# Expert rows in lanes of 32-row units: ten static rounds in place of eleven in a mixture-of-experts decoder trunk

## What is computed

```
scores = sigmoid(h @ w_router)                      # 512 x 16
group  = argmax over 4 groups of (sum of its two best biased scores)
expert = top_k(scores in that group, 2)             # 2 experts for each token
gate   = scores[expert] / sum(scores[expert])
counts = bincount(expert)                           # 1024 assignments over 16 experts
yb     = (silu(xb @ w_gate[e]) * (xb @ w_up[e])) @ w_down[e]   # xb: the rows of expert e
out[tok] += gate * yb
```

## Time and profile before

| what | us |
|---|---|
| three runs | 1645.20, 1642.72, 1634.35; median 1642.72 |
| the profiled execution | 1631.18 |
| its span, first to last instruction | 1629.4 |
| mixture of experts, layer 0: first round's first matmul to last down product's end | 653.3 to 934.4 |
| the same, layer 1 | 1315.0 to 1596.7 |
| spacing of the static rounds | 22.61 |

### The profile page before, as it was taken

The page is one execution under the profiler, slowest core; times in us unless marked ns, Lnnn a source line. Parts: engine busy times, 40 slices in busy tenths (PEclk is TensorE's granted clock), DMA queues, the critical chain, the costliest instruction groups (busy, mean ns, idle before and its releaser), DMA issues.

```text
span 1629.4 us, 22551 instructions
## 1 busy us (share of the span) xinstructions
PE 1434.7 (88%) x9837; PEld 743.0 (46%) x9837; DVE 674.6 (41%) x1044; ACT 306.5 (19%) x500; POOL 71.5 (4%) x199
## 2 busy tenths in 40 slices
PE   5999999967878797899999859969998789999992
PEld 3445565536666545433333344535654353333331
DVE  2114334235677316432333235785643543332334
ACT  2121211123342103100000042221112400000002
POOL 7000000000000000000000010000000000000001
PEclk9899999987999898999999979989999989999997
DMA  9686674031000007999997761201100599989884
GB/s 343 219 293 198 207 242 146 1 116 41 3 3 32 24 0 279 404 424 375 353 426 294 273 244 52 78 26 52 52 0 0 233 374 400 386 339 421 335 348 168
DMA packets 91215, 334.17 MB, mean 205 GB/s; under 512 B 6521, under 2 KB 37485, under 8 KB 74733
## 3 DMA queue, kind: packets, MB, share of 16 engines
q1 hardware_dynamic: 76880, 287.94, 46.4%
q10 hardware_dynamic: 8476, 23.82, 3.7%
q0 software_dynamic: 5760, 20.97, 3.4%
HBM read 309.65 MB, written 23.07 MB: 204 GB/s over the span
## 4 chain that ended last, share of the span: by engine, by line
PE 74%; DVE 14%; DMA 6%; ACT 4%; issue 2%; POOL 0%; DVEq 0%; SPq 0%; ACTq 0%; POOLq 0%
PE banks L1736 18%; PE banks L1284 14%; PE banks L1758 10%; PE banks L1656 5%; DVE work L1872 4%; PE banks L1325 4%; PE banks L1273 3%; PE banks L1220 3%; DMA work<-in_w_down_dram 2%; PE banks L1640 2%; PE banks L1719 1%; DVE work L1878 1%; DMA work<-h_rows,idx_tok 1%; PE banks L1450 1%; DMA ring<-in_w_ada_dram 1%
## 5 line engine op out<-in xcount | busy, mean ns | idle before, releaser
L1284 PE MATMUL banks<-h_features,ring 128*128 128x512 f32 (+1 forms) x656 | 291.3, 599 | 5.6 <-ACT h_features L897 4.0
L1736 PE MATMUL banks<-ring,work 128*64 128x512 f32 x672 | 231.3, 600 | 2.3 <-issue 2.3
L1736 PE MATMUL banks<-work 128*64 128x512 f32 x512 | 212.2, 595 | 0.0
L1284 PEld LDWEIGHTS banks<-h_features,ring 128*128 128x128 f32 (+1 forms) x656 | 121.4, 189 | 158.0 <-issue 154.3
L1872 DVE TENSOR_TENSOR work<-work,banks 128x256 f32<-128x256 f32 (+2 forms) x88 | 47.7, 564 | 190.6 <-PE banks L1736 144.7
L1758 PE MATMUL banks<-work 128*64 128x512 f32 x320 | 112.7, 593 | 0.0
L1872 DVE TENSOR_TENSOR work<-work 128x512 f32<-128x512 f32 (+9 forms) x202 | 100.2, 496 | 14.5 <-ACT work L1092 3.6
L1736 PEld LDWEIGHTS banks<-ring,work 128*64 128x64 f32 x672 | 72.1, 138 | 68.6 <-issue 63.9
L1758 PE MATMUL banks<-ring,work 128*64 128x512 f32 x256 | 98.4, 592 | 0.0
L1736 PE MATMUL banks<-h_features,work 128*64 128x512 f32 x192 | 89.5, 614 | 2.2 <-ACT work L1143 2.2
L1656 PE MATMUL banks<-y_features,ring 128*128 128x512 f32 x192 | 84.6, 603 | 6.4 <-DVE small L2404 6.4
(11 more groups left out here) (360 smaller groups left out, 1822.5 us busy)
## 6 DMA issues: line engine op xcount, KB each, us to landing
ring<-in_w_up_dram SPq DMA_DIRECT2D x16, 2048.0 KB, 13.0
y_features<-in_w_ada_dram SPq DMA_DIRECT2D x28, 1024.0 KB, 5.7
work<-in_w_down_dram SPq DMA_DIRECT2D x14, 2048.0 KB, 13.4
ring<-in_w_gate_dram SPq DMA_DIRECT2D x12, 2048.0 KB, 12.2
work<-in_w_up_dram SPq DMA_DIRECT2D x10, 2048.0 KB, 13.3
work<-in_w_gate_dram SPq DMA_DIRECT2D x10, 2048.0 KB, 12.7
ring<-in_w_ada_dram SPq DMA_DIRECT2D x8, 2048.0 KB, 12.2
h_features<-in_w_gate_dram SPq DMA_DIRECT2D x8, 2048.0 KB, 9.4
```

Source lines behind the costliest of these rows:

```text
L1284: ins = mm(PS[0:w, b, :], lhsT=W[:, k, c0:c0 + w], rhs=h[:, k, :], start=(k == 0), stop=(k == KD - 1))
L1736: ins = mm(PS[rows, bank, :], lhsT=xt[:, k, rows], rhs=ws[lane][:, k, :], start=(k == 0), stop=(k == KD - 1))
```

## The change

Lanes are cut in units of 32 rows. An expert takes 2, 3, 4 or 6 units in a row; a round still has 64 rows in each lane, that is two units. Where an expert has three units, the next one begins in the middle of a round: that lane's 64 rows then belong to two experts, 32 rows each. Places 1, 5, 6 and 7 hold 96 rows where they held 128; the others keep their capacities. The new tables have ten static rounds.

```diff
+QUARTER_ROWS = 32
-LANES = ([1, 1, 1, 1, 2, 1, 2, 2], [2, 3, 2, 1, 2, 1])
-ROUNDS = 11
+LANES = ([2, 2, 6, 2, 2, 4, 2], [3, 3, 2, 3, 3, 4, 2])
+ROUNDS = 10
...
+def place_numbers(u, n, lane):
+    lead = QUARTER_ROWS * (u % 2)
+    skip = -(lead + QUARTER_ROWS * n) % HALF_ROWS
+    return 2 * (u // 2) + lane, (lead + QUARTER_ROWS * n + skip) // HALF_ROWS, lead, skip
...
                 def weights(part, r):
-                    at = [home_of(part, r, lane) for lane in range(2)]
...
+                    parts = []
                     for lane in range(2):
+                        places = [place_at(2 * r + i, lane) for i in range(2)]
+                        width = HALF_ROWS if places[0] == places[1] else QUARTER_ROWS
+                        for i, place in enumerate(places[0:HALF_ROWS // width]):
+                            home = home_of(part, place)
+                            if PLACES[place][0] // 2 == r:
+                                pe.wait_ge(loaded[l][home], ...)
+                            p0 = HALF_ROWS * lane + QUARTER_ROWS * i
+                            parts.append((slice(p0, p0 + width), home_w(home, part)))
+                    return parts
...
                     for k in ks:
-                        for lane in range(2):
-                            rows = slice(64 * lane, 64 * lane + 64)
-                            ins = mm(PS[rows, bank, :], lhsT=xt[:, k, rows], rhs=ws[lane][:, k, :], start=(k == 0),
+                        for rows, w in ws:
+                            ins = mm(PS[rows, bank, :], lhsT=xt[:, k, rows], rhs=w[:, k, :], start=(k == 0),
                                      stop=(k == KD - 1))
...
-            for place, (r, n, lane) in enumerate(PLACES):
-                fill(place_of[:, 0, place:place + 1], float(2 * r + lane))
-                fill(place_of[:, 1, place:place + 1], float(n))
+            for place, run in enumerate(PLACES):
+                for i, number in enumerate(place_numbers(*run)):
+                    fill(place_of[:, i, place:place + 1], float(number))
...
-                pk = picked2.rearrange("p k (e n) -> p k e n", n=E)
-                link(tt(pk, bc(at_place, 2, 1), bc(place_of, E, 2), ALU.mult))
+                pk = picked4.rearrange("p k (e n) -> p k e n", n=E)
+                link(tt(pk, bc(at_place, 4, 1), bc(place_of, E, 2), ALU.mult))
                 link(dve.tensor_reduce(begin_runs, pk, AX_X, ALU.add))
+                begin, runs, lead, skip = [begin_runs[:, i, :] for i in range(4)]
+                link(tt(lead_skip, lead, skip, ALU.add))
+                link(stt(cap_rows, runs, float(HALF_ROWS), lead_skip, ALU.mult, ALU.subtract))
+                link(tt(count_led, cnt, lead_skip, ALU.add))
+                link(tt(cmp9, count_led..., bc(mult9, E, 1), ALU.is_gt))
...
+                link(tt(late, rank, bc(cap_rows, NT, 1), ALU.is_ge))
+                link(tt(placed, late, bc(skip, NT, 1), ALU.mult))
+                link(tt(placed, placed, rank, ALU.add))
+                link(tt(placed, placed, bc(lead, NT, 1), ALU.add))
+                link(tt(cmp8, f2(placed)..., bc(mult9[:, 1:9], NT * E, 1), ALU.is_ge))
```

More of the change, by code:

```diff
@@ L41, in lane_plan @@
     for lane, lengths in enumerate(LANES):
-        r = 0
+        u = 0
         for n in lengths:
-            runs.append((r, n, lane))
-            r += n
-        assert r == ROUNDS
+            runs.append((u, n, lane))
+            u += n
+        assert u == 2 * ROUNDS and lengths[-1] > 1
     first = [run for run in runs if run[0] == 0]
     rest = sorted((run for run in runs if run[0]), key=lambda run: (-run[1], run))
-    return first + rest + [(ROUNDS, 1, 0), (ROUNDS, 1, 1)]
+    return first + rest + [(2 * ROUNDS, 2, 0), (2 * ROUNDS, 2, 1)]
+def place_numbers(u, n, lane):
+    lead = QUARTER_ROWS * (u % 2)
+    skip = -(lead + QUARTER_ROWS * n) % HALF_ROWS
+    return 2 * (u // 2) + lane, (lead + QUARTER_ROWS * n + skip) // HALF_ROWS, lead, skip
 def phase_order():
@@ L63, in load_plan @@
     at = {phase: i for i, phase in enumerate(phase_order())}
-    loads = sorted((place > 1, at[part, r], lane, at[part, r + n - 1], place, part)
-                   for place, (r, n, lane) in enumerate(places) if r < ROUNDS for part in range(3))
+    loads = sorted((place > 1, at[part, u // 2], lane, at[part, (u + n - 1) // 2], place, part)
+                   for place, (u, n, lane) in enumerate(places) if u < 2 * ROUNDS for part in range(3))
     held = [-1] * 8
@@ L214, in trunk @@
         iota48 = small(2 * MAX_BLOCKS)
-        place_of = small(2, E)
+        place_of = small(4, E)
         first_two = small(E)
@@ L327, in trunk @@
         destf = ro(2, NT)
-        mult8 = ro(8)
+        mult9 = ro(9)
         tabf = ro(64)
@@ L438, in trunk, with place_at, home_of, last_home @@
         gathered = [[sem(f"l{l}_{j}_rows_gathered") for j in ("even", "odd")] for l in range(DEPTH)]
-        def home_of(part, r, lane):
-            place = [p for p, run in enumerate(PLACES) if run[2] == lane and run[0] <= r < run[0] + run[1]][0]
+        def place_at(u, lane):
+            return [p for p, run in enumerate(PLACES) if run[2] == lane and run[0] <= u < run[0] + run[1]][0]
+        def home_of(part, place):
             return [home for p, which, home, _ in LOADS if p == place and which == part][0]
+        def last_home(part, lane):
+            return home_of(part, place_at(2 * ROUNDS - 1, lane))
         def loads_of(home, last=None):
@@ L448, in loads_of @@
             return len(users) if last is None else users.index(last) + 1
-        IN_LOOP = [home_of(part, ROUNDS - 1, lane) for part in range(3) for lane in range(2)]
+        IN_LOOP = [last_home(part, lane) for part in range(3) for lane in range(2)]
+        assert len(set(IN_LOOP)) == 6
         loaded = [[sem(f"l{l}_home{i}_loaded" if i in IN_LOOP else f"home{i}_loaded") for i in range(8)]
@@ L1722, in weights @@
                 def weights(part, r):
[L1724 removed]
+                    parts = []
                     for lane in range(2):
[L1726 to L1729, removed]
+                        places = [place_at(2 * r + i, lane) for i in range(2)]
[3 more added lines that the diff above has]
+                            if PLACES[place][0] // 2 == r:
+                                pe.wait_ge(loaded[l][home], 16 * (loads_before(l, home) + loads_of(home, (place, part))))
+                            p0 = HALF_ROWS * lane + QUARTER_ROWS * i
+                            parts.append((slice(p0, p0 + width), home_w(home, part)))
+                    return parts
                 def lanes_up(bank, ws, xt, ks):
                     for k in ks:
[L1734 to L1736 removed]
+                        for rows, w in ws:
+                            ins = mm(PS[rows, bank, :], lhsT=xt[:, k, rows], rhs=w[:, k, :], start=(k == 0),
                                      stop=(k == KD - 1))
@@ L1755, in lanes_down @@
                         for n in range(2):
-                            for lane in range(2):
-                                rows = slice(64 * lane, 64 * lane + 64)
-                                ins = mm(PS[rows, 5 + n, :], lhsT=aT[:, k, rows], rhs=ws[lane][:, k, n * 512:(n + 1) * 512],
+                            for rows, w in ws:
+                                ins = mm(PS[rows, 5 + n, :], lhsT=aT[:, k, rows], rhs=w[:, k, n * 512:(n + 1) * 512],
                                          start=(k == 0), stop=(k == 3))
@@ L1790, in again @@
                     def again(part):
-                        for home in last[part]:
+                        homes_of = [last_home(part, lane) for lane in range(2)]
+                        for home in homes_of:
                             pe.wait_ge(loaded[l][home], (it + (loads_of(home) + 1)) * 16)
-                        return [home_w(home, part) for home in last[part]]
+                        return [(slice(HALF_ROWS * lane, HALF_ROWS * lane + HALF_ROWS), home_w(home, part))
+                                for lane, home in enumerate(homes_of)]
                     pe.wait_ge(sem(f"l{l}_xt_copied"), it + (ROUNDS + 1))
```

32 lines of the change are left out of this document (16 added, 16 removed).

## The result

The changed kernel takes 1707.05 us (median of four runs, 1704.88 to 1710.80), the kernel before, in the same measurements, 1643.96. The ratio is 1.039, 95% interval 1.034 to 1.044. That is 63 us more by the medians and 65 by the ratio. Forecast were 57.6 us more, 1700 us. Ratios in this document leave out two executions of later runs that took far longer than all others (3758 us in the run with places early and tokens first, 2136 us in the last run); the medians include them.

A forecast was written before the change was run, and what follows sets the result against it. The prediction took TensorE to bound the experts, 22.61 us a round. Two rounds less (-45.2), split rounds (+100.8) and routing (+2) sum to +57.6 on 1642.7: 1700 us, range 1600 to 1722, the likeliest case's own 1674 to 1725.

The forecast's parts named there:

- Two rounds less: Static expert rounds, 22 in place of 24 with the loop's passes counted: 22.61 us saved each, -45.2 us.
- The four split rounds: Rounds 1 and 5 of each layer: mixed widths do not overlap, a step takes 1.92 us, +100.8 us; chance 0.65.
- two ends: Three-matmul steps in split rounds: either all overlap at 0.87 us, costing 0, or each width change closes the array, +100.8 us.
- a distance of some 48 us between rounds: Sign expected in the profile after: starts of rounds 1 and 2, and of 5 and 6, this far apart, others 22.6.
- The routing: Longer VectorE work before round 1, 2.6 us more to the table of experts; +2 us together, bounds 0 and 6.
- home 7's load: Now holds weights needed at round 1's start; expected 2.1 us late in layer 0 and 1.0 in layer 1.
- the tokens' 0.9 us: Routing in layer 0: the tokens of the blocks come 0.9 us late, with the gather and round 1 behind them.
- The loads: 42 loads before the loop in ten rounds: with rounds 1 and 5 25 us longer, nothing waits.
- The term of the rival: If widths overlap, TensorE waits for loads at round 7: 2 us a layer, bounds 0 and 8.
- The sum: Whole kernel: -45.2 + 100.8 + 2 = +57.6 us, on the median 1642.7 giving 1700 us, 3.5% slower.
- the 5 us of the base: Allowance for the base in the likeliest case's own range, 1674 to 1725 us.
- The rival of overlapping widths: Split rounds: 64-wide and 32-wide matmuls overlap, splits are free; -39 us, 1604 us, 2.4% faster; chance 0.26.

The follow-up runs named there:

- the run with places early and tokens first: Changed kernel with four 32-wide matmuls in split rounds, experts' table for the places written early, blocks' tokens converted before the last tables: 0.973 of the kernel before, 1598.5 us.
- the last run: Against the run with tokens before tables, only other lanes, chosen so that by count no load comes late: 0.975 of the kernel before, 1600.8 us.
- the run with four 32-wide matmuls: Changed kernel, but in split rounds the unsplit lane is also two 32-wide matmuls, same weights twice: 0.979 of the kernel before, 1607.6 us.
- the run ordered by width: Changed kernel with the same three matmuls a step, but in each call all 64-wide ones first, then all 32-wide: 1.029 of the kernel before, 1688.9 us.
- the run with old lanes: Changed kernel with the lanes of the kernel before: eleven rounds, no split, old load order, new routing kept: 1.0026 of the kernel before.
- the run with tokens before tables: Four 32-wide matmuls in split rounds, lanes with splits in rounds 3 and 4, blocks' tokens converted before the last tables: 0.978 of the kernel before, 1603.7 us.

## Why the prediction was right, point by point

**Two rounds less, -45.2 us.** Right: 22 exponentials, ordinary rounds still at 22.6 us.

**The four split rounds, +100.8 us.** The mechanism was right, and was the choice between two ends. The size was short by 6: a step takes 1.98 us and not 1.92, 96 x (1.98 - 0.87) = 106.6. The missing 0.06 is in the records themselves: behind the first record after a change the next one starts not after 0.43 us, but after 0.48 if it is 64 wide (two span 1.07 us, of which the second is 0.59) and 0.45 if it is 32 wide (694.67 to 695.12). The larger part could have been read in the kernel before, where the first 64-wide matmuls after the 128-wide transposes start at 736.63 and 737.11. The run with four 32-wide matmuls took the 107 us away; the run ordered by width divided them, 12 phases x 6.98 = 84 us for the overlap and about 20 for the changes. What stayed open before, whether a 64-wide matmul and 32-wide ones in disjoint columns overlap, is settled: they don't. The sign of a distance of some 48 us between rounds didn't come in that form, because a split round's down product falls into the next round: the up products of rounds 4, 5 and 6 start at 791.43, 822.89 and 863.37, that is 31.5 and 40.5 us apart where ordinary ones are 22.6, together 26.7 us for one split round:

```profile
791.43 16.79 PE banks L1761 x62
...
822.89 20.32 PE banks L1761 x68
...
863.37 11.31 PE banks L1761 x52
```

**The routing, +2 us.** VectorE's chain grew by 2.64 us to the table (662.52 - 655.94 against 657.23 - 653.29) and the tokens came 0.96 later; predicted were 2.6 and 0.9. Round 1 began 2.4 us later in layer 0 and 0.7 in layer 1: 3.1, predicted 2, within its bounds. The amount is right, but the cause only in one layer. The prediction took its 2 us from home 7's load. In layer 0 that load landed 13.6 us after 664.91, some 0.5 us before round 1 began, and the chain goes through the gather, which was slower than before (12.0 us for 11.2) and issued later; in layer 1 the chain goes through home 7's load, and round 1 begins with its landing (below). That the sum came out near is in part luck: the run with old lanes shows 1.4 to 2.0 us a layer of waiting for the gather alone, for which the prediction had only the tokens' 0.9 us.

```profile
1364.55 13.46 DMA y_features<-in_w_gate_dram
1378.15 12.33 PE banks L1761 x30
```

**The loads.** Apart from home 7's at the start of round 1, nothing waited for them in the static rounds, as said for this case. The term of the rival, 2 us a layer at round 7, was of the right order for these lanes (some 1 us in the run with four 32-wide matmuls) and not for others (7).

**The sum**: -45.2 + 106.6 + 3.1 = 64.5, beside 66.8 in the experts of the profiled executions and 65 by the ratio of the runs. The remaining 2 of the profile lie in two places. The four split rounds together are 108.1 us longer than ordinary ones, 1.5 more than 106.6, most of it in round 1, where the first matmuls after the wait run at a lower granted clock (0.82 and 0.80). And the loop's pass of layer 1 is 1.0 us longer, where its down weights took 16.74 us for 15.72. The prediction's own range has a slip: its lower end takes the 5 us of the base off, its upper end doesn't add them. With them it is 1674 to 1730; 1707 lies in either.

**The rival of overlapping widths** gave 1604 us, 2.4% faster; what the split rounds' other form reached is 1607.6, 2.1%. Its sum came near for the kernel in which widths don't mix within a step, though its terms differ: less waiting at round 7 (0.8 us in layer 0), more at the start of round 1.

## What to carry to other kernels

Matmuls that are to share the array should all have one width: here three of mixed widths cost more than twice what four equal ones cost (1.98 us and 0.87 a step), and cutting a wide one in two with the same weights cost nothing. A packing change should be priced by what one step of it takes on TensorE and not by the number of rounds that it saves. Where a small gather and large loads become ready together, try the gather first: it was worth 0.6% in the kernel before, and nothing where the round waited for the load anyway.

## What wasn't expected of the hardware

- Four 32-wide matmuls of 512 columns run at the pace of two 64-wide ones to the digit, 6.87 us for eight steps of each.
- A change of width costs 0.10 us before the next matmul, and another 0.05 (to 64) or 0.02 (to 32) in it.
- A late gather costs more than its wait. After the wait the granted clock is lower, and round 1's first 20 records take 6.1 to 6.9 us (6.21 at 0.73 in the kernel before) where they take 4.5 at 1.00 when there is next to no wait (the run with tokens before tables).
- An indirect gather of 128 rows of 4 KB took 4.2 to 4.8 us to land when it was issued 1.3 to 1.4 us ahead of a run of 2 MiB loads, the loads before having landed, and 11 to 12.5 us when it came 0.5 us or more behind the first of that run. Whether it is the order in the DMA engines or their sharing that costs the time was not tried apart.
